# Four of twelve conditioning pieces scaled by ScalarE and summed by GpSimd in place of multiplied by TensorE

## The chip, the cores and the metric

The kernel runs on one core of a Trainium2 chip, in one launch. The metric is the device time of that launch in microseconds. Five engines work side by side and meet through semaphores: TensorE (matrix multiplication), VectorE, ScalarE, GpSimd, and SyncE (SP), which here only issues transfers. Each takes its own instructions in order.

## What is computed

A decoder layer over 512 tokens of width 1024, batch 1, all in float32:

```python
cond = silu(c)                                   # (1, 1024)
ada = cond @ w_ada + b_ada                       # (1, 6144)
sh1, sc1, g1, sh2, sc2, g2 = split(ada, 6)
h = rms_norm(x, norm1_g) * (1 + sc1) + sh1
q, ckv, qi, ki, wi, a_pool, gate_a, gate_b = split(h @ w_in)
o_a = sparse_attention(q, ckv, qi, ki, wi)       # top 128 keys of each query
o_b = multiscale_pool(a_pool, w_pool)
merged = sigmoid(gate_a) * (o_a @ w_a_up) + sigmoid(gate_b) * (o_b @ w_b_up)
x = x + g1 * (merged @ w_out)
h2 = rms_norm(x, norm2_g) * (1 + sc2) + sh2
x = x + g2 * moe(h2)                             # 4 of 32 experts
out = rms_norm(x, final_g)
```

The line that the change touches is `ada = cond @ w_ada`: one row times a 1024 x 6144 matrix. It is cut into twelve pieces of 512 columns, a0 to a11. Pieces 0 to 3 (shift and scale of the first norm) are needed at once; 4 to 11 make g1, sh2, sc2 and g2, which are used only after the attention stage. Pieces 8 to 11 are those changed.

## The kernel before

The work of every engine is written out by hand, in one list for each. TensorE's results go through the eight banks of PSUM: a list JOBS gives each result its number n and its bank n mod 8, and a job may start when the eighth job before it has been emptied (function start). An entry says who empties it, "A" ScalarE or "D" VectorE.

Weights of the first half come in pieces of 2 MB through four ring buffers in the order of PIECES, issued by SP. A piece is issued when the one before it in the same buffer has been used (function used). For a conditioning piece that is when its job is done. Because SP issues in order, a piece that waits holds all behind it. Around the change the order is a8, a9, gb1, a10, a11, wb (w_b_up), ga0, ga1, wa; a9, a10, a11 and ga0 share one buffer, and gb1 follows a8 in another.

The attention stage is a loop over eight groups g, two for each chunk of 128 queries (four heads each). In group g TensorE does, in this order: turned probabilities PT (L1617, four jobs), scores L of group g+1 (L1603), O(g) (probabilities times the latent, in L1480), the matmuls of gate part gb(g+1) (24 of them, in L1480), in group 0 the pooling product z (L1631), in odd groups V (L1480), in group 1 the row sums of pieces 4 to 7 (L1593), and in groups 0 to 3 a conditioning piece, ada_part(8 + g) at L1511. ScalarE copies the turned probabilities (L895) and O (L906), takes exponentials of group g+1 (L880), the tanh of the gate (L884), rounds the gate weights after the next into a high part (L821), and then copies z (L913), V (L916) and the conditioning result (L806). GpSimd makes the low part of those gate weights (L619); VectorE does the maxima (L1159), the top-k search, and scales the probabilities (L1193).

ada_part multiplies a piece with the conditioning vector in 8 matmuls, 32 columns wide, and leaves partial sums in 128 rows; a later sum over the rows with a matrix of ones (ada_sum) makes the row of 512 values, and ada_rows adds the bias. After the stage come the B branch, gate a with the A branch, the output projection, and the experts.

Of the kernel before, what the change touches and what calls it, by code (L numbers as in the profile page):

```python
# [24 lines left out]
ACT = mybir.ActivationFunctionType  # L25
# [5 lines left out]
KD = D // P  # L31
# [34 lines left out]
def trunk(nc, x, c, norm1_g, norm2_g, w_ada, b_ada, w_in, kv_norm_g, w_uk, w_uv, w_pool, pool_scale,  # L66
# [3 lines left out]
    with ctx:  # L70
# [3 lines left out]
        def sem(name):  # L74
            return ctx.enter_context(nc.semaphore(name))
# [12 lines left out]
        T3 = sb("T3", [P, 3, T])  # L88
# [16 lines left out]
        cnd = sb("cnd", [P, 3, KD])  # L105
# [159 lines left out]
        NGR = 2 * C  # L265
        JOBS += [("L", i, "D") for i in range(4)] + [("gb", 0, "A")]
        for g in range(NGR):
            JOBS += [("PT", 4 * g + i, "A") for i in range(4)]
            if g < NGR - 1:
                JOBS += [("L", 4 * g + 4 + i, "D") for i in range(4)]  # L270
            JOBS += [("O", g, "A")]
            if g < NGR - 1:
                JOBS += [("gb", g + 1, "A")]
            if g == 0:
                JOBS += [("z", i, "A") for i in range(PG)]
            if g % 2:
                JOBS += [("V", g // 2, "A")]
            if g == 1:
                JOBS += [("row", j, "D") for j in range(4, 8)]
            if g < 4:  # L280
                JOBS += [("ada", 8 + g, "A")]
        JOBS += [("B", m, "D") for m in range(KD)]
        JOBS += [("row", j, "D") for j in range(8, 12)]
        JOBS += [("ga", 0, "A")]
# [26 lines left out]
        zo_hi_ok, zo_lo_ok = sem("zo_hi_ok"), sem("zo_lo_ok")  # L311
        b_hi_ok, b_lo_ok = sem("b_hi_ok"), sem("b_lo_ok")
        c_ok = sem("c_ok")
        job_done = sem("job_done")
        by_act, by_vec = sem("by_act"), sem("by_vec")
        c_in, x_in, sv_in, kvg_in = sem("c_in"), sem("x_in"), sem("sv_in"), sem("kvg_in")
# [81 lines left out]
        def front_came(eng, kind, i=0):  # L398

            n = place[kind, i]  # L400
            eng.wait_ge(piece_in[slot_of[n]], 16 * (slot_of[:n + 1].count(slot_of[n])))
# [22 lines left out]
        def buffer_free(eng, kb):  # L424

            if turn_no[kb] >= 2:
# [3 lines left out]
                else:  # L430
                    eng.wait_ge(job_done, number[kind, m] + 1)

        def up_w_block(kind, m):
            return piece("wb" if kind == "B" else "wa")[:, :, m * P:(m + 1) * P]

# [14 lines left out]
        def _(sp):  # L450
# [6 lines left out]
            def used(n):  # L457

                kind, i, _ = PIECES[n]
                if kind == "a":  # L460
                    sp.wait_ge(job_done, number["ada", i] + 1)
                elif kind in ("wb", "wa"):
                    sp.wait_ge(u_lo_ok, KD if kind == "wb" else 2 * KD)
                elif kind in ("q", "pool", "gb", "ga"):
                    sp.wait_ge(b_lo_ok, block_no[LAST_JOB[kind, i]] + 1)
                else:
                    sp.wait_ge(job_done, number[LAST_JOB[kind, i]] + 1)
# [82 lines left out]
        def _(pool):  # L550
# [65 lines left out]
            def block_low(n):  # L616

                pool.wait_ge(b_hi_ok, n + 1)
                nc.gpsimd.tensor_tensor(wb_hl[:, buffer_of(BLOCKS[n]), 1, :, :], block_w(n),  # L619
                                        wb_hl[:, buffer_of(BLOCKS[n]), 0, :, :],  # L620
                                        ALU.subtract).then_inc(b_lo_ok, 1)
# [25 lines left out]
            for half in range(2):  # L647
                pool.dma_start(ada_half[half],
                               b_ada[0, 2 * D:6 * D].rearrange("(r a n) -> r a n", r=4, a=2)[:, half, :]
                               ).then_inc(brow_in, 16)  # L650
            for n in range(block_no["gb", 2], block_no["ga", 0]):
                block_low(n)
            pool.wait_ge(job_done, number["V", C - 1] + 1)

            for part in range(3):
# [117 lines left out]
        def _(act):  # L773
# [30 lines left out]
            def ada_copy(j):  # L804

                nc.scalar.activation(acc[j], job("ada", j), ACT.Copy).then_inc(by_act, 1)  # L806
# [65 lines left out]
            index_chunk(3)  # L872
            ada_copy(7)

            def exponentials(g):
                n = P * (g // 2 + 1)
                for i in range(4):
                    s = 4 * g + i
                    act.wait_ge(max_ok, s + 1)
                    nc.scalar.activation(Lt[:, i, 0:n], Lt[:, i, 0:n], ACT.Exp, scale=SCALE,  # L880
                                         bias=am[:, 1, s:s + 1], accum_out=am[:, 2, s:s + 1]).then_inc(exp_ok, 1)
# [8 lines left out]
            for g in range(NGR):  # L890
                ch, hh = g // 2, g % 2
                n = P * (ch + 1)
                for i in range(4):
                    src = job("PT", 4 * g + i)
                    nc.scalar.activation(pT[:, 0:ch + 1, i, :], src[:, 0:n].rearrange("p (s q) -> p s q", q=P),  # L895
                                         ACT.Copy).then_inc(by_act, 1)
                if g == NGR - 1:
                    act.wait_ge(job_done, number["L", 4 * NGR - 1] + 1)
                    for k in range(PG):
                        last = nc.scalar.activation(zo_hl[:, 0, k, :], zT[:, k, :], ACT.Copy)  # L900
                    last.then_inc(zo_hi_ok, 1)
                    up_high("B", 0)
                    up_high("B", 1)
                if g == 0:
                    act.wait_ge(d_ok, PG)
                nc.scalar.activation(o_latT[:, 4 * hh:4 * hh + 4, :].rearrange("p h q -> p (h q)"),  # L906
                                     job("O", g), ACT.Copy).then_inc(by_act, 1)
                if g < NGR - 1:
                    exponentials(g + 1)
                    gate_b(g + 1)  # L910
                if g == 0:
                    for i in range(PG):
                        nc.scalar.activation(zT[:, i, :], job("z", i), ACT.Copy,  # L913
                                             scale=svT[:, 24 + i:25 + i]).then_inc(by_act, 1)
                if hh:
                    nc.scalar.activation(oT[:, :, ch * P:(ch + 1) * P],  # L916
                                         job("V", ch).rearrange("p (a q) -> p a q", a=4),
                                         ACT.Copy).then_inc(by_act, 1)
                if g < 4:
                    ada_copy(8 + g)  # L920

            for m in range(2, KD):
                up_high("B", m)
# [122 lines left out]
        def _(dve):  # L1046
# [8 lines left out]
            def job(kind, i=0):  # L1055
                dve.wait_ge(job_done, number[kind, i] + 1)
                return bank(kind, i)

            v = nc.vector
# [81 lines left out]
            def ada_rows(j):  # L1141

                r, half = (j - 4) // 2, (j - 4) % 2
                row = small[32 * r:32 * r + 1, 1536 * half:1536 * half + CH]
                v.tensor_tensor(row, job("row", j)[32 * r:32 * r + 1, :], row, ALU.add).then_inc(by_vec, 1)

            last_scores = relu[:, 1, :]
# [309 lines left out]
        def _(pe):  # L1458
# [26 lines left out]
            def emptied_by(kind, i=0):  # L1485

                n = number[kind, i]
                pe.wait_ge(by_act if JOBS[n][2] == "A" else by_vec, emptied[n])
# [100 lines left out]
            def ada_sum(j):  # L1589

                b_ = start("row", j)
                emptied_by("ada", j)
                mm(b_, ones[:, :], acc[j], start=True, stop=True).then_inc(job_done, 1)  # L1593

# [15 lines left out]
            for g in range(NGR):  # L1611
                ch, hh = g // 2, g % 2
                for i in range(4):
                    b_ = start("PT", 4 * g + i)
                    pe.wait_ge(prob_ok, 4 * g + i + 1)
                    for s in range(ch + 1):
                        last = nc.tensor.transpose(b_[:, s * P:(s + 1) * P], Lt[:, i, s * P:(s + 1) * P], ident[:, :])  # L1617
                    last.then_inc(job_done, 1)
                if g < NGR - 1:
                    logits(g + 1)  # L1620
                b_ = start("O", g)
                emptied_by("PT", 4 * g + 3)
                chain(b_, [(ckv[:, s, :], pT[:, s, :, :].rearrange("p h q -> p (h q)")) for s in range(ch + 1)], job_done)
                if g < NGR - 1:
                    gate_b(g + 1)
                if g == 0:
                    pe.wait_ge(pool_in, 16)
                    for i in range(PG):
                        b_ = start("z", i)
                        pe.wait_ge(d_ok, i + 1)  # L1630
                        mm(b_, wpool[:, i, :], dT[:, i, :], start=True, stop=True).then_inc(job_done, 1)  # L1631
                if hh:
                    b_ = start("V", ch)
                    pe.wait_ge(uv_in, 16 * H)
                    emptied_by("O", g)
                    for a in range(4):
                        last = chain(b_[:, a * P:(a + 1) * P],
                                     [(uvp[:, 2 * a + q, :], o_latT[:, 2 * a + q, :]) for q in range(2)])
                    last.then_inc(job_done, 1)
                if g == 1:  # L1640
                    for j in range(4, 8):
                        ada_sum(j)
                if g < 4:
                    ada_part(8 + g)

            def branch(kind, m):

# [293 lines left out]
```

## Time and profile before

| | us |
|---|---|
| median of 3 runs | 997.53 (996.18 to 999.67) |
| the profiled execution, its own time | 998.4 |
| its span in the profile | 996.6 |
| TensorE busy | 956.7 (96%) |
| VectorE busy | 404.5 (41%) |
| ScalarE busy | 227.2 (23%) |
| GpSimd busy | 191.3 (19%) |

The span runs from the first to the last instruction of one execution; the 1.8 us around it are in the time but not in the span. Busy time of TensorE counts matmuls as they stream through and says little on how full they are. The attention stage lies between about 125 and 234 us of the span, the experts fill it from about 410 on.

### The profile page before, as it was taken

The page shows a single profiled execution, that of the slowest core. Times are in us where ns is not written, and L with a number is a line of the kernel's source. Part 1 is how long each engine was busy: PE and PEld are TensorE (multiplying, and loading weights), DVE is VectorE, ACT ScalarE, POOL GpSimd, SP SyncE. Part 2 cuts the span into 40 slices and gives each one's busy share as a digit, 9 for nine tenths or more (in the row PEclk, how much of TensorE's full clock was granted, in tenths as well). Part 3 has the DMA queues.
Part 4 walks back from the last instruction along what each step waited for, and adds up shares of the span by engine and source line. Part 5 has one row for each costly group of instructions (what it writes and reads, how often), then busy time and mean ns, then how long its engine had stood idle before and what let it go on. Part 6 is the DMA issues. An engine that isn't in the chain of part 4 may idle for free.

```text
span 996.6 us, 17022 instructions
## 1 busy us (share of the span) xinstructions
PE 956.7 (96%) x7199; PEld 517.7 (52%) x7199; DVE 404.5 (41%) x833; ACT 227.2 (23%) x488; POOL 191.3 (19%) x238
## 2 busy tenths in 40 slices
PE   3899989999999999899999999999999999999995
PEld 2676656767788746544444444443444444344442
DVE  0275967744533565323432323223232323223245
ACT  6334354443322323110010101011010101101012
POOL 2223941004200001212121111212111121211000
PEclk9999999999999999999999999999999999999998
DMA  9927623620422657989999999999999999999915
GB/s 338 341 86 253 229 84 122 242 85 16 170 85 96 242 231 262 349 301 375 377 348 372 390 387 385 389 386 397 372 397 385 388 389 379 386 370 393 381 37 182
DMA packets 71443, 283.96 MB, mean 285 GB/s; under 512 B 7488, under 2 KB 8796, under 8 KB 54984
## 3 DMA queue, kind: packets, MB, share of 16 engines
q1 hardware_dynamic: 61720, 257.93, 67.3%
q0 software_dynamic: 9648, 24.94, 9.5%
q8 instruction: 58, 0.95, 0.4%
q14 instruction: 17, 0.14, 0.0%
HBM read 272.62 MB, written 18.56 MB: 292 GB/s over the span
## 4 chain that ended last, share of the span: by engine, by line
PE 87%; DMA 5%; DVE 3%; issue 2%; ACT 1%; SPq 1%; POOL 0%; POOLq 0%; DVEq 0%; ACTq 0%
PE ps L1744 22%; PE ps L1480 20%; PE ps L1775 11%; PE ps L1755 11%; PE ps L1766 5%; PE ps L1692 2%; DMA ring<-in_w_ada_dram 2%; PE ps L1703 2%; PE ps L1731 2%; PE ps L1603 2%; PE ps L1532 2%; PE ps L1842 2%; PE ps L1511 1%; PE ps L1739 1%; DMA apad<-h_rows,iug 1%
## 5 line engine op out<-in xcount | busy, mean ns | idle before, releaser
L1317 DVE TENSOR_SCALAR mix<-ps 128x384 f32<-128x384 f32 x32 | 17.9, 558 | 288.3 <-ACT attn L980 288.3
L1480 PE MATMUL ps<-h_hi,wb_hl 128*128 128x512 f32 x384 | 126.0, 402 | 0.0
L700 POOL DMA_INDIRECT moe_rows<-mix,ius x31 | 47.8, 1543 | 249.4 <-DVE mix L1362 248.5
L1358 DVE SCALAR_TENSOR_TENSOR mix<-ps,WC,attn 64x512 f32<-64x512 f32 x64 | 47.9, 748 | 103.3 <-PE ps L1775 102.8
L980 ACT ACTIVATE attn<-ps 128x384 f32<-128x384 f32 x32 | 15.7, 491 | 309.1 <-PE ps L1755 309.1
L1480 PEld LDWEIGHTS ps<-h_hi,wb_hl 128*128 128x128 f32 x384 | 72.2, 188 | 19.7 <-issue 4.4
L1480 PE MATMUL ps<-h_lo,wb_hl 128*128 128x512 f32 x192 | 74.8, 389 | 0.0
L1362 DVE SCALAR_TENSOR_TENSOR mix<-ps,WC,attn 32x256 f32<-32x256 f32 x128 | 61.5, 481 | 1.9
L1744 PE MATMUL ps<-ring,mix 128*64 128x512 f32 x272 | 59.9, 592 | 0.0
L1744 PE MATMUL ps<-ring,uvp 128*64 128x512 f32 x256 | 59.0, 609 | 0.0
L619 POOL TENSOR_TENSOR wb_hl<-ring,wb_hl 128x1024 fp32r<-128x1024 f32 x16 | 38.5, 2415 | 85.1 <-ACT wb_hl L821 68.8
L1775 PE MATMUL ps<-ring,attn 128*64 128x512 f32 x240 | 54.8, 598 | 0.0
L992 ACT ACTIVATE attn<-ps 128x384 f32<-128x384 f32 x32 | 15.7, 491 | 168.2 <-PE ps L1842 168.2
L1480 PE MATMUL ps<-zo_hl,wb_hl 128*128 128x512 f32 x192 | 44.9, 389 | 0.0
L1480 PEld LDWEIGHTS ps<-h_lo,wb_hl 128*128 128x128 f32 x192 | 36.2, 189 | 9.1 <-issue 2.2
L1480 PEld LDWEIGHTS ps<-zo_hl,wb_hl 128*128 128x128 f32 x192 | 36.0, 188 | 7.4
L730 POOL COPY ius<-idx 128x1 uint32 (+1 forms) x31 | 7.8, 252 | 156.7 <-DMA moe_rows<-mix,ius 156.7
L1744 PEld LDWEIGHTS ps<-ring,mix 128*64 128x64 f32 x272 | 19.0, 137 | 35.3 <-issue 34.7
L694 POOL DMA_INDIRECT apad<-h_rows,iug x32 | 32.0, 999 | 25.2 <-POOL iug L721 24.4
L1744 PEld LDWEIGHTS ps<-ring,uvp 128*64 128x64 f32 x256 | 18.4, 141 | 34.7 <-issue 34.2
L821 ACT ACTIVATE wb_hl<-ring 128x1024 fp32r<-128x1024 f32 x24 | 25.2, 1052 | 38.5 <-PE ps L1480 32.6
L1775 PEld LDWEIGHTS ps<-ring,attn 128*64 128x64 f32 x240 | 15.9, 136 | 31.9 <-issue 31.9
(305 smaller groups left out, 1540.6 us busy)
## 6 DMA issues: line engine op xcount, KB each, us to landing
ring<-in_w_gu_dram SPq DMA_DIRECT2D x66, 1024.0 KB, 19.0
ring<-in_w_down_dram SPq DMA_DIRECT2D x30, 1024.0 KB, 13.5
ring<-in_w_ada_dram SPq DMA_DIRECT2D x12, 2048.0 KB, 11.9
area_b<-in_w_gu_dram SPq DMA_DIRECT2D x16, 1024.0 KB, 17.9
hT<-in_w_gu_dram SPq DMA_DIRECT2D x16, 1024.0 KB, 19.6
X<-in_w_gu_dram SPq DMA_DIRECT2D x16, 1024.0 KB, 18.9
area_a<-in_w_gu_dram SPq DMA_DIRECT2D x14, 1024.0 KB, 19.3
ring<-in_w_in_dram SPq DMA_DIRECT2D x6, 2048.0 KB, 7.9
```

The lines of the kernel that those rows point to most:

```text
L619: nc.gpsimd.tensor_tensor(wb_hl[:, buffer_of(BLOCKS[n]), 1, :, :], block_w(n), wb_hl[:, buffer_of(BLOCKS[n]), 0, :, :], ALU.subtract).then ...
L694: pool.indirect_dma_start(out=XG[0:slots, b, :], out_offset=None, in_=h2_dram, in_offset=bass.IndirectOffsetOnAxis(ap=iug[0:slots, b:b + 1 ...
L700: pool.indirect_dma_start(out=y_dram, in_=Y[0:slots, b, :], in_offset=None, out_offset=bass.IndirectOffsetOnAxis(ap=which, axis=0), bounds ...
L821: nc.scalar.activation(wb_hl[:, buffer_of(BLOCKS[n]), 0, :, :], block_w(n), ACT.Copy).then_inc(b_hi_ok, 1)
L1358: v.scalar_tensor_tensor(out=Y[0:SA, b, sl], in0=ps[SA * g:SA * (g + 1), 2, :], scalar=WC[0:SA, w:w + 1], in1=g2b[0:SA, sl], op0=ALU.mult, ...
L1362: last = v.scalar_tensor_tensor(out=Y[SA:slots, b, sl], in0=ps[SB * j:SB * (j + 1), 3, 0:2 * P], scalar=WC[SA:slots, w:w + 1], in1=g2b[SA: ...
L1480: last = mm(out_, a, b, start=(n == 0 and start_), stop=(n == len(pairs) - 1))
L1532: last = mm(b_[:, 0:TOKW], hT[:, k, ch * P:(ch + 1) * P], w[:, k, :], start=(k == 0), stop=(k == KD - 1))
L1744: mm(ps[SA * g:SA * (g + 1), 0, :], xgT[b][:, k, 0:SA], w[:, k % 2, g, :, :, :], start=False, stop=(k == KD - 1), tile_position=(0, SA * g))
L1755: last = mm(ps[SB * j:SB * (j + 1), 1, 0:2 * P], xgT[b][:, k, SA:slots], w[:, k % 2, j // 2, j % 2, :, :], start=False, stop=(k == KD - 1) ...
L1766: mm(ps[SB * j:SB * (j + 1), 3, 0:2 * P], actT[:, 2, SB * k:SB * (k + 1)], w[:, k % 2, 2 * P * j:2 * P * (j + 1)], start=(k == 0), stop=(k ...
L1775: last = mm(ps[SA * g:SA * (g + 1), 2, :], actT[:, k % 2, SA * (k // 2):SA * (k // 2) + SA], w[:, k % 2, g * CH:(g + 1) * CH], start=(k == ...
```

## The change

Pieces 8 to 11 are no longer multiplied by TensorE. Each consists of 8 parts of 128 x 512 (part k holds the rows of w_ada that partition p meets with value k of the conditioning vector). ScalarE multiplies a part by its column of the conditioning vector into one of two buffers in T3 (scale_parts), and GpSimd copies the first and adds the others into acc (add_parts). Scaling n waits until part n-2 has been added. In group 0 all eight parts of a8 are done, in each of groups 1 to 6 four parts. The sum over rows stays on TensorE, now waiting for GpSimd. The vector holds 1/32 of the values, so the row is multiplied by 32 in ada_rows.

```diff
-            if g < 4:
-                JOBS += [("ada", 8 + g, "A")]
...
+        SCALED = [[(8, k) for k in range(KD)]] + [[(9 + g // 2, 4 * (g % 2) + i) for i in range(4)] for g in range(6)]
+        scaled = [T3[:, 1 + i, :] for i in range(2)]
...
-                if kind == "a":
+                if kind == "a" and i >= 8:
+                    sp.wait_ge(scaled_ok, KD * (i - 7))
+                elif kind == "a":
                     sp.wait_ge(job_done, number["ada", i] + 1)
...
-            for n in range(block_no["gb", 2], block_no["ga", 0]):
-                block_low(n)
+            def add_parts(which):
+
+                for j, k in which:
+                    n = (j - 8) * KD + k
+                    pool.wait_ge(scaled_ok, n + 1)
+                    if k:
+                        pool.wait_ge(part_ok, n)
+                        last = nc.gpsimd.tensor_tensor(acc[j], scaled[k % 2], acc[j], ALU.add)
+                    else:
+                        last = nc.gpsimd.tensor_copy(acc[j], scaled[k % 2])
+                    last.then_inc(part_ok, 1)
+
+            block_low(block_no["gb", 2])
+            for g in range(NGR - 1):
+                if g + 3 < KD:
+                    block_low(block_no["gb", g + 3])
+                add_parts(SCALED[g])
...
+            def scale_parts(which):
+
+                for j, k in which:
+                    n = (j - 8) * KD + k
+                    front_came(act, "a", j)
+                    if n >= 2:
+                        act.wait_ge(part_ok, n - 1)
+                    nc.scalar.activation(scaled[k % 2], piece("a", j)[:, k, :], ACT.Copy,
+                                         scale=cnd[:, 2, k:k + 1]).then_inc(scaled_ok, 1)
...
+                if g < NGR - 1:
+                    scale_parts(SCALED[g])
                 if hh:
                     nc.scalar.activation(oT[:, :, ch * P:(ch + 1) * P],
                                          job("V", ch).rearrange("p (a q) -> p a q", a=4),
                                          ACT.Copy).then_inc(by_act, 1)
-                if g < 4:
-                    ada_copy(8 + g)
...
-                emptied_by("ada", j)
+                if j < 8:
+                    emptied_by("ada", j)
+                else:
+                    pe.wait_ge(part_ok, KD * (j - 7))
                 mm(b_, ones[:, :], acc[j], start=True, stop=True).then_inc(job_done, 1)
...
-                if g < 4:
-                    ada_part(8 + g)
```

ScalarE in the order of its list, before, from the gate of group 0 to the probability copies of group 2 (attn<-ps with 128x128 or 128x2x128 is L895; mix is the gate, wb_hl the high part, apad the V copy, area_b the z and conditioning copies):

```order
L884 ACTIVATE mix<-ps 128x512 [waits job_done]
L821 ACTIVATE wb_hl<-ring 128x1024 [waits job_done,piece_in0]
L913 ACTIVATE area_b<-ps,svT 128x512 [waits job_done] x4
L806 ACTIVATE area_b<-ps 128x512 [waits job_done]
L895 ACTIVATE attn<-ps 128x128 [waits job_done] x4
L906 ACTIVATE attn<-ps 128x512 [waits job_done]
L880 ACTIVATE attn,am<-attn,am 128x256 [waits max_ok] x4
L884 ACTIVATE mix<-ps 128x512 [waits job_done]
L821 ACTIVATE wb_hl<-ring 128x1024 [waits job_done,piece_in1]
L916 ACTIVATE apad<-ps 128x4x128 [waits job_done]
L806 ACTIVATE area_b<-ps 128x512 [waits job_done]
L895 ACTIVATE attn<-ps 128x2x128 [waits job_done] x4
```

The same place of ScalarE's list after the change (T<-ring,cnd is a scaling; line numbers have moved, L913 is the old L884, L924 the old L895):

```order
L913 ACTIVATE mix<-ps 128x512 [waits job_done]
L840 ACTIVATE wb_hl<-ring 128x1024 [waits job_done,piece_in0]
L942 ACTIVATE area_b<-ps,svT 128x512 [waits job_done] x4
L901 ACTIVATE T<-ring,cnd 128x512 [waits piece_in1] x2
L901 ACTIVATE T<-ring,cnd 128x512 [waits part_ok,piece_in1] x6
L924 ACTIVATE attn<-ps 128x128 [waits job_done] x4
L935 ACTIVATE attn<-ps 128x512 [waits job_done]
L909 ACTIVATE attn,am<-attn,am 128x256 [waits max_ok] x4
L913 ACTIVATE mix<-ps 128x512 [waits job_done]
L840 ACTIVATE wb_hl<-ring 128x1024 [waits job_done,piece_in1]
L901 ACTIVATE T<-ring,cnd 128x512 [waits part_ok,piece_in2] x4
L947 ACTIVATE apad<-ps 128x4x128 [waits job_done]
```

Eight scalings, and in later groups four, now stand ahead of the V copy and the probability copies; all but the first two wait for GpSimd (part_ok).

GpSimd before, from the end of pooling to the expert biases (wb_hl is the low part of the gate weights):

```order
L641 TENSOR_TENSOR area_b<-area_b,apad 128x512 [waits pool_chain]
L648 DMA small<-in_b_ada_dram 4x512 [waits job_done,select_ok]
L648 DMA small<-in_b_ada_dram 4x512
L619 TENSOR_TENSOR wb_hl<-ring,wb_hl 128x1024 [waits b_hi_ok] x6
L656 DMA T<-in_b_gu_dram 32x1024 [waits job_done]
```

GpSimd after, the same place (area_b<-T is the copy, area_b<-T,area_b the additions):

```order
L652 DMA small<-in_b_ada_dram 4x512
L623 TENSOR_TENSOR wb_hl<-ring,wb_hl 128x1024 [waits b_hi_ok] x2
L664 COPY area_b<-T 128x512 [waits scaled_ok]
L662 TENSOR_TENSOR area_b<-T,area_b 128x512 [waits part_ok,scaled_ok] x7
L623 TENSOR_TENSOR wb_hl<-ring,wb_hl 128x1024 [waits b_hi_ok]
L664 COPY area_b<-T 128x512 [waits scaled_ok]
L662 TENSOR_TENSOR area_b<-T,area_b 128x512 [waits part_ok,scaled_ok] x3
L623 TENSOR_TENSOR wb_hl<-ring,wb_hl 128x1024 [waits b_hi_ok]
L662 TENSOR_TENSOR area_b<-T,area_b 128x512 [waits part_ok,scaled_ok] x4
```

The six low parts stood alone in the list; now additions stand between them, and a group's low part comes ahead of its additions.

## Rows read from the trace of the kernel before

**Rows 1.** The page's first part: busy us, share of the span, instructions.
```profile
PE 956.7 (96%) x7199; PEld 517.7 (52%) x7199; DVE 404.5 (41%) x833; ACT 227.2 (23%) x488; POOL 191.3 (19%) x238
```
**Rows 2.** Busy us by stretch of the span, attention stage; then PEclk, DMA share, GB/s.
```profile
core 0: us, PE busy (x) PEld busy (x) DVE busy (x) ACT busy (x) POOL busy (x), PEclk, DMA share, GB/s
140.00:230.00 90.00, 89.01 (x425) 59.34 (x424) 52.83 (x164) 42.78 (x106) 15.46 (x8) 1.00 0.40 141
```
**Rows 3.** The chain that ended last, attention stage: start us, us, what.
```profile
142.22 1.85 PE ps L1511 x16
...
144.66 1.73 PE ps L1603 x8
146.39 8.13 PE ps L1480 x42
...
162.56 7.18 PE ps L1480 x28
169.74 1.85 PE ps L1511 x16
...
175.20 8.96 PE ps L1480 x44
...
190.06 8.05 PE ps L1480 x30
198.11 1.31 PE ps L1617 x12
...
202.85 9.81 PE ps L1480 x46
...
217.85 8.93 PE ps L1480 x32
226.80 0.60 ACT mix L884
...
229.50 3.69 PE ps L1480 x8
```
**Rows 4.** ScalarE in order of time: start us, us, engine, line, what [idle before].
```profile
140.26 1.84 ACT L913 ACTIVATE area_b<-ps,svT 128x512 f32<-128x512 f32 x3
...
144.63 0.78 ACT L895 ACTIVATE attn<-ps 128x128 f32<-128x128 f32 x4
...
169.78 0.60 ACT L884 ACTIVATE mix<-ps 128x512 f32<-128x512 f32 x1 [2.90 <-PE ps L1480]
170.27 1.05 ACT L821 ACTIVATE wb_hl<-ring 128x1024 fp32r<-128x1024 f32 x1
...
172.15 1.21 ACT L895 ACTIVATE attn<-ps 128x256 f32<-128x256 f32 x4
...
227.30 2.06 ACT L895 ACTIVATE attn<-ps 128x512 f32<-128x512 f32 x4
```
**Rows 5.** GpSimd in order of time, group 0.
```profile
144.02 4.72 POOL L619 TENSOR_TENSOR wb_hl<-ring,wb_hl 128x1024 fp32r<-128x1024 f32 x2
```
**Rows 6.** Three lines of GpSimd: duration ns min/median/max, first and last start, forms.
```profile
L641 POOL TENSOR_TENSOR area_b<-area_b,apad x4: 1272/1297/1600, 103.4 to 129.4; 128x512 f32<-128x512 f32 x4
L635 POOL TENSOR_TENSOR attn<-attn x6: 1039/1041/1264, 108.2 to 127.1; 128x512 f32<-128x512 f32 x6
L639 POOL TENSOR_SCALAR area_b<-attn x4: 607/607/872, 102.7 to 128.7; 128x496 f32<-128x496 f32 x4
```
**Rows 7.** Transfers issued from 138 to 230: KB each, median us to landing.
```profile
ring<-in_w_in_dram SPq DMA_DIRECT2D x3, 2048.0 KB, 7.8
```
**Rows 8.** TensorE in order of time ahead of group 0.
```profile
127.30 0.30 PE L1617 MATMUL ps<-ident,attn 128*128 128x128 f32 x1 [2.11 <-DVE attn L1193]
128.56 0.70 PE L1617 MATMUL ps<-ident,attn 128*128 128x128 f32 x2 [0.96 <-DVE attn L1193]
```
**Rows 9.** TensorE by stretch: us, busy, granted clock, DMA share, GB/s.
```profile
130.00:140.00 10.00, 10.00 (x38) 0.83 0.01 2
420.00:430.00 10.00, 9.32 (x36) 0.66 1.01 381
```
**Rows 10.** VectorE in order of time, group 1.
```profile
154.72 2.25 DVE L1193 TENSOR_SCALAR attn<-attn,am 128x256 f32<-128x256 f32 x1
```

More of the change, by code:

```diff
@@ L313, in trunk @@
         c_ok = sem("c_ok")
+        part_ok, scaled_ok = sem("part_ok"), sem("scaled_ok")
         job_done = sem("job_done")
@@ L1144, in ada_rows @@
                 row = small[32 * r:32 * r + 1, 1536 * half:1536 * half + CH]
-                v.tensor_tensor(row, job("row", j)[32 * r:32 * r + 1, :], row, ALU.add).then_inc(by_vec, 1)
+                v.scalar_tensor_tensor(out=row, in0=job("row", j)[32 * r:32 * r + 1, :], scalar=(32.0 if j >= 8 else 1.0),
+                                       in1=row, op0=ALU.mult, op1=ALU.add).then_inc(by_vec, 1)
             last_scores = relu[:, 1, :]
```

## Prediction

> **What bounds the kernel now.** I read the busy shares first: TensorE is busy 956.7 of 996.6 us [rows 1], and 89.01 of the 90 us between 140 and 230, where the attention stage lies [rows 2]. A busy share alone does not say that TensorE sets the end, so I read the chain that ended last through this stage [rows 3]: from 142 on its pieces are TensorE work, and only at 226.80 does ScalarE come into it. So TensorE time taken out here comes off the end, and a wait goes onto it. After the stage the order of work is fixed and its weight loads are released by the same jobs, so I take a shift of the stage as a shift of the end, one for one.
>
> Then the two engines that get the work. ScalarE is busy 42.78 of those 90 us and GpSimd 15.46 [rows 2]: by totals there is room. What counts is where in a group the work stands, since both take their instructions in order. In group g, ScalarE finishes the gate of group g+1 (L884, then the high part L821) and then copies the turned probabilities (L895), and TensorE cannot start O without these copies. The time from the end of the gate matmuls to O is where the change will be felt; I call it the turnaround. For O(3) it is 169.74 to 175.20, 5.46 us: 1.85 for a conditioning piece, 3.6 for transposes and scores [rows 3].
>
> **What is removed.** Four multiplications of a conditioning piece, 1.85 us each on the chain [rows 3]: 7.4 us. Four copies of their results on ScalarE go too; ScalarE was waiting for TensorE there, so I count nothing.
>
> **What is added, and its prices.** 32 scalings on ScalarE of 128x512 with a scale per partition. The nearest row is L913 (from PSUM, same shape, same kind of scale), three in 1.84 us, each overlapping the next [rows 4]; I take 0.55. On GpSimd 28 additions of 128x512 and 4 copies. The addition reads two different tiles and writes one of them, as L641 does (median 1.297); L635 reads one tile twice and takes 1.041 [rows 6]. I take 1.29 plus 0.08 between dependent instructions, 1.37, and 1.13 as the low end. The f32 copy is not in the trace: L639, a one-input form of 496 elements, takes 0.607 [rows 6]; I take 0.75 with its gap.
>
> The Trainium skill, GPSIMD Engine Reference, sections 3.1 and 4.1, speaks against this move: it sends two-input elementwise work to VectorE because GpSimd pays about 2.6 cycles an element. An estimate from that page, 512 elements at 1.2 GHz, is 1.11 us, between the two rows; with it (and the same gap) the sum below would be 2.3 us smaller.
>
> **The hold.** There are two scaling buffers, so the third scaling of a group waits for the first addition, the fourth for the second. GpSimd begins each group up to 4 with its own low part L619, 2.4 us [rows 5], which waits for the same high part. And the scalings stand ahead of the next probability copies on ScalarE. So behind the waiting scaling are queued the V copy and the four L895 copies, hence O, hence the next gate on TensorE. On SP the gb1 piece, and all behind it, now waits for the eighth scaling.
>
> Group 0 has eight parts. GpSimd does two low parts from 144.02 to 148.74 [rows 5], the copy to 149.5, then an addition every 1.37: the sixth part ends at 156.35. The eighth scaling waits for it and ends at 157.05; four copies (0.78 [rows 4]) end at 157.8, and O(1) starts at 157.95. It was 146.39 [rows 3]: **+11.6**, the removed multiplication of this group already in it.
>
> For the others I set the new turnaround against the old. Group 2 to O(3): from the gate's end 0.12 to ScalarE, gate copy 0.5, high part 0.95 (from the starts and durations at 169.78 and 170.27 [rows 4]), low part 0.1 + 2.4, two additions 2.74, 0.1 + 0.55 for the last scaling, copies 4 x 0.30, 0.15 to TensorE: 8.8. Old 5.46: **+3.35**. Group 4 to O(5): the copies are 4 x 0.41 (between 0.30 at width 256 and 0.515 at 512 [rows 4]), so 9.25; old 202.85 - 198.11 = 4.74 [rows 3]: **+4.5**. Group 6 to O(7): no low part, no scores. 0.12 + 0.5, scalings with their waits 0.55 + 0.1 + 2.74 + 0.1 + 0.55 = 4.04, copies 2.06, 0.15: 6.9. The old gate ended about 226.7 and O began at 229.50, 2.8: **+4.1**.
>
> Odd groups have the V turn, about 1.85, which covers part. O plus gate took 7.18 from O(2) and 8.05 from O(4) [rows 3], which gives the ends of the odd gates: 152.7, 182.4, 210.9. Group 3 to O(4): here the first part is the shorter copy, so the last scaling ends 6.85 after the gate; V copy 0.5, copies 1.64, 0.15: 9.15. Old 190.06 - 182.4 = 7.7: **+1.5**. Group 1 to O(2): again 6.85 and V copy 0.5; then one transpose that needs the bank of V (with the ada jobs gone, the eighth job before it is V), 0.33, and scores 1.73 [rows 3]: 9.4. The gb1 piece, released at 157.1 and not at 144.07, lands 8 to 8.5 later (7.8 in the trace [rows 7]) and holds the high part 0.7 more: 10.1. Old 162.56 - 152.7 = 9.9: **+0.25**. Group 5 to O(6): no low part, copies ready after 6.75; TensorE itself took 217.85 - 210.9 = 6.95: **0**.
>
> Sum: 11.6 + 0.25 + 3.35 + 1.5 + 4.5 + 0 + 4.1 = **+25.3**, the saved 7.4 included. On this path lie 13 additions (5, 1, 2, 1, 2, 0, 2), so 0.1 us on one moves the end 1.3.
>
> **The clock.** TensorE waited 2.11 and 0.96 us around 127 to 129 [rows 8], and the granted clock then averaged 0.83 from 130 to 140: 3.4 us at the lower level (1.2 GHz), a loss of 1.7. Around 420 the mean was 0.66 over ten, 6.8 us at that level, a loss of 3.4 [rows 9]. After the change TensorE waits 13.4 us before O(1) (scores done at 144.5), and 5.2, 4.5 and 5.1 before O(3), O(5) and O(7). I take the smaller loss four times, 6.8, since it lies in this stage, less the 0.7 of the gb1 piece, which the slower matmuls hide: **+6.1**. The ends of this term are 0 and 13.
>
> 25.3 + 6.1 = +31.4. On the profiled execution's 998.4 us that is 1029.8; the median of the three runs is 997.53, 0.9 lower, so I forecast **1029 us**.
>
> **Costed at nothing.** The row sum at L1145 gets another form of the same size, off the chain. The a10, a11 and ga0 loads are each released one or more groups later, but each has 13 us or more until its use; a load over that would add its excess once. w_b_up is issued behind a11 and has about 25 us.
>
> **Rivals.**
> *It fits by totals.* 32 scalings are 17.6 us against 47 idle on ScalarE, the additions 41 against 74 idle on GpSimd [rows 2]; TensorE stays the bound and gains 7.4: 990.1. Group 2 decides: TensorE needs 3.6 for transposes and scores, ScalarE 2.9 without a hold, so a hold under 0.7 costs nothing and one over 2.5 eats the saving. I count 5.9. Even free additions would leave group 0 with six scalings behind the low parts: O(1) at 153.1, +6.7. Chance 0.02; no change 0.01.
> *The hold without the clock.* The waits stand, but the clock drops once or not at all: 1019.5 (25.3 less 3.1 for quick additions) to 1025. Only two drops stand in the trace, so that each wait brings one is not shown. Chance 0.22.
> *Contention.* One probability scaling on VectorE took 2.25 us, its neighbours about 0.35, while a GpSimd subtraction ran [rows 10]. Meeting GpSimd's additions could do this in each group, or stretch the additions: at 1.6 each the sum is 13 x 0.23 = 3 more, 1032. Against it: GpSimd adds right behind the gate, when VectorE is past these scalings. With four clock losses of 3.4 it is 1036. Chance 0.2 for both.
> *The likeliest*, four waits with four short drops, 1025 to 1033: 0.55.
>
> The Trainium skill, Advanced Engine Details and Errata, VectorE Performance Modes, Mode Summary, notes that VectorE's second port is shared with GpSimd and that two-port forms and GpSimd block each other. The 2.25 us row agrees.
>
> The range 1018 to 1038 takes in quick additions without a clock loss and the long clock losses. A difference under 0.3% could not be told from none here: slower 0.97, same 0.01, faster 0.02.
>
> **What would show it.** Right: TensorE waits for the probability copies about 13 us before O(1) and 4 to 6 before O(3), O(5), O(7), about none before O(6); ScalarE waits for GpSimd's additions; additions of about 1.3; clock at the lower level for some us after these waits. Wrong: additions far from 1.3, no wait before O(5) and O(7), a wait over 2 us on a late piece, or later stages that take part of the shift back.

## The result and the profile after

| | median us | lowest to highest | ratio to before, 95% interval |
|---|---|---|---|
| before, same chip | 997.6 | 996.2 to 999.7 | |
| after | 1041.0 | 1039.2 to 1044.4 | 1.0435 [1.0409, 1.0462] |

The change costs 43.4 us. I had forecast 1029, with 1038 as the upper end: the sign was right, and 12 us were missing. The profiled execution took 1044.43 us, 46 more than the one of before, so I look for some 46 us in the trace.

First the page's busy shares of after, as in [rows 1]: busy us, share of the span, instructions.
```profile
PE 966.9 (93%) x7135; PEld 523.4 (50%) x7135; DVE 403.9 (39%) x833; ACT 245.7 (24%) x516; POOL 227.2 (22%) x270
```
TensorE has 64 matmuls fewer and is still busy 10 us longer; the lower granted clock shown below accounts for it. The other 36 us of the span are waits and stops. No engine got full: ScalarE gained 18.5 us and GpSimd 35.9, and both are still mostly idle.

The waits of TensorE in the attention stage of after: who waited for whom, us in total, times, longest.
```profile
PE ps L1510 <- ACT attn L924: 28.9, 5, 13.5
PE ps L1636 <- ACT apad L947: 2.3, 1, 2.3
PE ps L1650 <- ACT apad L947: 1.5, 1, 1.5
PE ps L1510 <- ACT attn L935: 0.8, 1, 0.8
```
L924 is the probability copy (L895 of before), L947 the V copy, L1510 the products of O, L1636 the scores and L1650 the transposes; the last row, V(3) behind the copy of O(7), is 0.8 in the kernel before too. Where the waits stand shows in TensorE's own order of time (after; start us, us, what, in brackets the idle time ahead and its releaser). These are the starts of O(1), O(3), the late scores of group 3, and O(4) to O(7):
```profile
159.01 2.05 PE L1510 MATMUL ps<-attn,ckv 128*128 128x512 f32 x2 [13.52 <-ACT attn L924]
192.57 3.75 PE L1510 MATMUL ps<-attn,ckv 128*128 128x512 f32 x4 [5.14 <-ACT attn L924]
209.23 0.91 PE L1636 MATMUL ps<-T,hT 128*128 128x384 f32 x2 [2.31 <-ACT apad L947]
210.84 5.46 PE L1510 MATMUL ps<-attn,ckv 128*128 128x512 f32 x6 [0.70 <-ACT attn L924]
231.22 5.46 PE L1510 MATMUL ps<-attn,ckv 128*128 128x512 f32 x6 [4.39 <-ACT attn L924]
249.29 3.60 PE L1510 MATMUL ps<-attn,ckv 128*128 128x512 f32 x8
265.27 6.75 PE L1510 MATMUL ps<-attn,ckv 128*128 128x512 f32 x8 [5.15 <-ACT attn L924]
```
O(1), O(3), O(5) and O(7) wait for the copies, O(6) doesn't. Eight products of O take 3.60 us at O(6) and 6.75 at O(7): same work, at half the clock (the granted clock from 265 to 272 is 0.54).

The chain that ended last says what the copies were late for. Group 0 of after:
```profile
147.48 2.30 POOL wb_hl L623
149.78 0.56 POOL area_b L664
...
150.47 1.28 POOL area_b L662
...
151.89 1.28 POOL area_b L662
...
156.12 1.27 POOL area_b L662
...
157.48 0.72 ACT T L901
158.20 0.68 ACT attn L924 x4
...
159.01 8.16 PE ps L1510 x26
```
Where [rows 3] had TensorE alone, there now stand GpSimd's low part (L623), its copy (L664), five additions (L662), ScalarE's eighth scaling (L901) and its four copies. The additions start 1.41 us apart, 1.27 of it busy.

The clock behind three of the waits, by stretch (after; us, TensorE busy, granted clock as a share of 2.4 GHz, DMA share, GB/s):
```profile
190.00:195.00 5.00, 2.43 (x3) 0.50 0.43 131
195.00:200.00 5.00, 5.00 (x19) 0.86 0.79 288
210.00:215.00 5.00, 4.30 (x6) 0.50 0.01 3
215.00:220.00 5.00, 5.00 (x18) 0.81 0.00 0
230.00:235.00 5.00, 3.79 (x5) 0.55 0.78 253
235.00:240.00 5.00, 5.00 (x16) 0.77 1.01 369
```
From each start of O until its matmuls quicken, TensorE runs at 1.2 GHz: 3.2 us at O(1), 3.8 at O(3), 6.8 from the late scores of group 3 on, 6.1 at O(5), 6.2 at O(7). Half of each is lost: 1.6, 1.9, 3.4, 3.0 and 3.1, together 13.0 us.

The last piece lies nowhere near the change. TensorE ahead of its last 16 matmuls (the last expert's combine), before:
```profile
979.95 7.11 PE L1914 MATMUL ps<-mix,small 128*128 128x512 f32 x16 [0.52 <-DVE mix L1362]
```
and after:
```profile
1023.77 9.81 PE L1945 MATMUL ps<-mix,small 128*128 128x512 f32 x16 [4.59 <-issue]
```
A stop of 4.6 us, where it was 0.5, that no semaphore explains ("issue"), then 2.7 us more for the same matmuls: 6.8 us in all.

**The balance.** From the start of z to group 7's V products the stage took 95.3 us before and 133.1 after, +37.7; it began 1.1 later in this execution. Up to the reading of the last rows (977.54, now 1017.01) the shift is 39.5, up to the first output write (986.82, now 1032.89) 46.1. So the long expert stage gives nothing back, and the tail adds 6.6. In the stage TensorE's waits add up to 32.7 (the rows above and the 1.5 at L1650), where before had one of 1.0 ahead of O(7); less that and the 7.4 of the removed multiplications it is 24.3. Of the 37.7 then 13.4 are left for the clock; the stretches gave 13.0.

### The profile page after: what moved, and what is told of

Read it like the earlier page. It is cut to its first block, busy times and chain, and to the rows that moved or that the text cites. A ratio compares the mean times of both kernels' runs of the same rounds, so it can differ in the third digit from the quotient of the medians.

```text
span 1042.7 us, 17008 instructions
## 1 busy us (share of the span) xinstructions
PE 966.9 (93%) x7135; PEld 523.4 (50%) x7135; DVE 403.9 (39%) x833; ACT 245.7 (24%) x516; POOL 227.2 (22%) x270
## 4 chain that ended last, share of the span: by engine, by line
PE 81%; issue 5%; POOL 4%; DMA 4%; DVE 3%; ACT 2%; SPq 1%; DVEq 0%; POOLq 0%; ACTq 0%
PE ps L1775 21%; PE ps L1510 18%; PE ps L1806 11%; PE ps L1786 10%; PE ps L1797 5%; PE ps L1723 2%; POOL area_b L662 2%; PE ps L1762 2%; DMA ring<-in_w_ada_dram 2%; PE ps L1734 2%; PE ps L1562 2%; PE ps L1873 1%; POOL wb_hl L623 1%; DMA apad<-h_rows,iug 1%; PE ps L1770 1%
## 5 line engine op out<-in xcount | busy, mean ns | idle before, releaser
L1510 PE MATMUL ps<-h_hi,wb_hl 128*128 128x512 f32 x384 | 129.0, 410 | 0.0
L1510 PEld LDWEIGHTS ps<-h_hi,wb_hl 128*128 128x128 f32 x384 | 73.7, 192 | 21.2 <-issue 5.5
L1510 PE MATMUL ps<-h_lo,wb_hl 128*128 128x512 f32 x192 | 75.6, 394 | 0.0
L1510 PE MATMUL ps<-attn,ckv 128*128 128x512 f32 x40 | 30.9, 926 | 28.9 <-ACT attn L924 28.9
L623 POOL TENSOR_TENSOR wb_hl<-ring,wb_hl 128x1024 fp32r<-128x1024 f32 x16 | 38.4, 2407 | 83.3 <-ACT wb_hl L840 66.3
L1510 PE MATMUL ps<-zo_hl,wb_hl 128*128 128x512 f32 x192 | 44.9, 389 | 0.0
L1510 PEld LDWEIGHTS ps<-h_lo,wb_hl 128*128 128x128 f32 x192 | 36.9, 192 | 10.4 <-issue 3.3
L1510 PEld LDWEIGHTS ps<-zo_hl,wb_hl 128*128 128x128 f32 x192 | 35.9, 188 | 7.4
L662 POOL TENSOR_TENSOR area_b<-T,area_b 128x512 f32<-128x512 f32 x28 | 35.5, 1267 | 14.6 <-ACT T L901 11.0
## 6 DMA issues: line engine op xcount, KB each, us to landing
ring<-in_w_gu_dram SPq DMA_DIRECT2D x66, 1024.0 KB, 18.5
```

Of the source, the lines that this page charges most:

```text
L662: last = nc.gpsimd.tensor_tensor(acc[j], scaled[k % 2], acc[j], ALU.add)
L1510: last = mm(out_, a, b, start=(n == 0 and start_), stop=(n == len(pairs) - 1))
```

## The experiments

T in the expectations is the theory that GpSimd's additions hold ScalarE and so O, and that the clock behind the waits costs the rest. Medians are compared with runs of the kernel before on the same chip; "stage" is the stretch from the start of z to group 7's V products, 95.3 us before. hum issues short bf16 matmuls whose results nobody reads, 0.12 to 0.13 us each. In the last four expectations T is another theory, which each of them states.

**Again.** The changed kernel, unaltered.

> The changed kernel once more, for its profile. Theory T (the hold: probability copies queued behind scalings that wait for GpSimd, plus clock losses of 13 us, plus a tail of up to 6 us): the waits before O(1), O(3), O(5), O(7) are again 13.5, 5.1, 4.4 and 5.1 us within 0.3, since they follow from fixed durations; the stretches at the lower clock differ by some us in place and length; the wait of 4.6 us of TensorE before the last 16 matmuls either stands again (then it belongs to the program) or is near 0.5 (then it varies by execution). Time 1037 to 1045. Rival (the waits themselves vary, for instance through transfers): one of the four waits differs by more than 1 us.

Measured: 1040.3, ratio 1.0416 [1.0377, 1.0455]; the waits before O are 13.51, 5.12, 4.39 and 5.15, the stage takes 133.0, the stop ahead of the combine 4.8, and the matmuls behind it 8.58 where they had taken 9.81. Waits, drops and the stop belong to the program, not to one execution; the clock behind the stop varies.

**Short matmuls in the waits.** If the clock falls because TensorE idles, work without a use should keep it up.
```diff
+                hum(b_, {1: 100, 3: 36, 5: 30, 7: 36}.get(g, 0))
```
This stands directly ahead of O(g), in O's own bank.

> The changed kernel with short matmuls without use in TensorE's waits before O(1), O(3), O(5), O(7) (100, 36, 30, 36 of about 0.12 us). The waits stay as long as they are, so only the clock changes. Theory T (the lower clock behind the waits costs 13 us, 3.4 of it behind the wait at O(4), which is not filled): 9 to 10 us less, 1031, and a granted clock near 1.00 from 159 to 200. Rival (the clock term is what I predicted, 6 us, and the remainder is something else): 4 to 5 us less, 1036.

Measured: 1044.6, ratio 1.0454 [1.0412, 1.0496]; no gain, where I had expected 1031. The trace says why (TensorE, in order of time):
```profile
158.13 12.95 PE L1506 MATMUL ps<-ones,onesb 128*128 128x256 bf16 x100 [12.93 <-ACT attn L924]
...
278.54 3.70 PE L1510 MATMUL ps<-attn,ckv 128*128 128x512 f32 x8 [1.14 <-ACT attn L924]
```
O's bank is the one that the probability copy empties, so the short matmuls waited for the same copy and then came on top: 12.95, 5.77 and 6.25 us in groups 1, 3 and 5. Only those of group 7, whose bank was free, lay in the wait, and there the eight products of O took 3.70 instead of 6.75. The stage is 143.6 us, 10.6 longer than in the repeat; the time doesn't show it because the stop ahead of the combine is 0.5 us in this kernel. So I put the others into a bank that VectorE had long emptied:
```diff
+                    if g == 5 and i == 3:
+                        pe.wait_ge(by_vec, emptied[number["L", 4 * g]])
+                        hum(bank("L", 4 * g), 12)
...
+                if g in (1, 3, 5):
+                    pe.wait_ge(by_vec, emptied[number["L", 4 * g + 4]])
+                    hum(bank("L", 4 * g + 4), {1: 100, 3: 30, 5: 24}[g])
...
+                if g == 7:
+                    hum(b_, 38)
```

> The changed kernel with matmuls without use in all five waits of TensorE (before O(1) 100, O(3) 30, the last score ahead of O(4) 12, O(5) 24, O(7) 38, 0.12 us each), now in a bank that VectorE has just emptied, so that they stand inside the waits. In the run before, three of the four groups of them had waited for the probability copies themselves, and only those before O(7) filled a wait: there the clock stayed at 1.00 and O(7) to V took 4.5 us, not 7.5. Theory T (13.0 us are lost to the lower clock in the stage: 1.6, 1.9, 3.4, 3.0, 3.1): the V of group 7 starts 11 to 13 us earlier, at 260 to 262 and not 272.8, clock near 1.00 from 160 on; the time 1026 to 1031, by the wait near the end. Rival (the clock follows its own course, whatever TensorE does in the waits): V at 268 or later.

Measured: 1023.3, ratio 1.0248 [1.0224, 1.0272], less than the 1026 to 1031 expected. The clock by stretch, in this kernel:
```profile
150.00:160.00 10.00, 7.36 (x67) 0.97 0.01 2
160.00:170.00 10.00, 10.00 (x44) 0.86 0.60 210
170.00:180.00 10.00, 8.54 (x33) 1.00 0.01 2
...
200.00:210.00 10.00, 8.30 (x53) 1.00 0.01 4
...
220.00:230.00 10.00, 8.22 (x39) 1.00 0.31 98
```
All drops but the first are gone, and the stage is 122.4 us, 10.6 less than in the repeat, though the copies come no sooner (O(1) starts 19.3 us behind z in both). The rest of the gain of 17 us fits the tail: here the combine comes after 0.5 us. So the clock was worth about 11 us with one drop of 1.4 (10 us at 0.86) left: 12 in all.

**Additions ahead of the low part on GpSimd.**
```diff
+                add_parts(SCALED[g])
                 ...
-                add_parts(SCALED[g])
```
The first stands ahead of block_low, the second behind it.

> The changed kernel with GpSimd's additions of a group ahead of its low part (in group 0 one low part still comes first). Theory T (the hold holds the low part's 2.4 us): 2.4 less before O(1), 1.9 less before O(2) to O(5) each, about 9.6 in all, and up to 3 more where a shorter wait no longer lowers the clock: V of group 7 at 260 to 264, 1028 to 1033. Rival (the low part would run beside the first scalings anyway and adds nothing): less than 3 us.

Measured: 1023.1, ratio 1.0258 [1.0240, 1.0275], the stage 116.6; 5 us less than the low end of what I expected. The waits are 11.21, 3.46, 0.59 with 0.70, 2.69 and 5.15, and none is left before O(2): 8.9 us less. The gain in the stage is 16.5, since between 170 and 240 the clock never falls either, behind these shorter waits:
```profile
180.00:190.00 10.00, 6.54 (x26) 1.00 0.20 68
...
210.00:220.00 10.00, 7.31 (x28) 1.00 0.23 70
```
The hold is GpSimd's, and its low part was 9 us of it. The 7.6 us beyond that are what the shorter waits gave back of the clock, more than twice the 3 us that I had allowed for.

**No additions.** GpSimd only copies the last part; the other seven of each piece stay out of the sum, and ScalarE waits for nothing of GpSimd's but that one copy of a piece.
```diff
+                    if k < KD - 1:
+                        continue
+                    pool.wait_ge(scaled_ok, KD * (j - 7))
+                    nc.gpsimd.tensor_copy(acc[j], scaled[1]).then_inc(part_ok, 1)
...
-                        act.wait_ge(part_ok, n - 1)
+                        act.wait_ge(scaled_ok, n - 1)
```

> The changed kernel with the additions left out: GpSimd copies only the last scaled part of each piece, so the four rows are sums over one part in eight; the 32 scalings stay where they are and wait for none of GpSimd's work but one copy a piece. Theory T (the wait for the additions is the cost, the scalings' own time the rest): the holds shrink to 4 x 0.63 (8 x 0.63 in group 0): O(1) near 150.5 after scores at 145.3, O(3), O(5), O(7) with waits of 2 to 3, at most one or two clock drops: 1003 to 1009. Rival (scalings on ScalarE in themselves cost most): over 1020.

Measured: 1007.5, ratio 1.0109 [1.0076, 1.0142], the stage 102.5. What is left are the scalings themselves, which stand ahead of the probability copies on ScalarE: 4.25 us of wait before O(1), 1.71, 0.50, 0.94 and 3.42 before O(3), O(4), O(5) and O(7).
```profile
148.60 2.04 PE L1508 MATMUL ps<-attn,ckv 128*128 128x512 f32 x2 [4.25 <-ACT attn L922]
```
So ScalarE's waiting for GpSimd, for its low part as well as its additions and with the clock that this costs, is 30.6 of the stage's 37.7 us. The waits left are 10.8 us, 1.0 of them there before. That alone is 2.4 more than the 7.4 saved, and the remaining 4.8 of the 7.2 us by which this stage is still longer than before are left for the clock. A kernel with eight scaling buffers in place of two, which would have shown what the hold costs with all additions still made, has no room in SBUF beside the other tensors and was not measured.

**The four pieces left out.** The kernel before, without their multiplications and copies; the row sums then go over other data, and SP issues the load behind each of these pieces when it has landed and a gate part is done (not shown).
```diff
-            if g < 4:
-                JOBS += [("ada", 8 + g, "A")]
...
-                if g < 4:
-                    ada_copy(8 + g)
...
-                if g < 4:
-                    ada_part(8 + g)
```

> The kernel before with the multiplications of pieces 8 to 11 and their copies left out and nothing in their place; the pieces are still loaded, and the four rows are sums over other data. It prices what is taken from TensorE alone. Theory (TensorE is the bound in groups 0 to 3): 4 x 1.85 = 7.4 less, less 0.5 to 1 where the probabilities come late: 991 (990 to 993), if the end of the kernel is as before. Rival (VectorE's search is nearly the bound, so most of the saving turns into waits for probabilities): 994 to 996, with waits of TensorE for L1193 of 3 us or more.

Measured: 996.7, ratio 0.9987 [0.9968, 1.0006], where I had expected 991 with an unchanged end. The stage is 6.3 us shorter (7.4 saved, with a new wait of 1.3 for GpSimd's low part), but the end has changed:
```profile
974.74 9.83 PE L1912 MATMUL ps<-mix,small 128*128 128x512 f32 x16 [5.46 <-issue]
```
The stop at the tail has come with it, into a kernel that puts nothing of these pieces on ScalarE or GpSimd. So it is no matter of the scalings. All five kernels with the stop (after, its repeat, the additions first, no additions, the pieces left out; 4.2 to 5.5 us) have 64 matmuls and 64 weight loads fewer than before: everything behind stands 128 instructions earlier. The two with short matmuls in the waits, which have about 200 matmuls more, don't have it. The next three runs test that place in the program.

**64 short matmuls at the start.** One line at the program's start (they run from 2.0 to 11.1 us, while the first loads are under way) puts the 128 instructions back; applied to after, before, and the kernel without the pieces.
```diff
+            hum(bank("sv"), 64)
```

> The changed kernel with 64 short matmuls without use at the very start of TensorE's list, where TensorE waits for the first transfers, which costs nothing there; it moves all later instructions by 128 places. Theory T (part of the change's cost is where its instructions fall against the blocks in which they are loaded): the wait falls to 0.5, the matmuls behind it run at the upper clock, and the time falls by 4 to 7 us, to 1034 to 1037. Rival (the wait is a result of what the engines do at the end, or of the clock): the wait stays over 4 us and the time within 1 us.

> The kernel before with the same 64 short matmuls at the start. Removing pieces took 128 instructions from the list and brought the wait near the end; if blocks are 256 instructions long, adding 128 puts the end at the same place within a block. Theory T: the wait of 4 to 5.5 us appears in the unchanged kernel, 4 to 7 us slower, 1002 to 1005. Rival (the pads' position means nothing): no change, the wait at 0.5.

> The kernel with pieces 8 to 11 not multiplied (rows are sums over other data) and 64 short matmuls at the start. Its stage was already 6.4 us shorter, its time only 1.0 us less, with a wait of 5.5 near the end. Theory T: the wait falls to 0.5 and the time to 990 to 992, which shows the full price of the removed multiplications. Rival: stays at 995 to 997.

| | without, us (ratio to before) | with 64, us (ratio to before) | stop ahead of the combine, us |
|---|---|---|---|
| after | 1041.0 [1.0409, 1.0462] | 1034.5 [1.0342, 1.0394] | 4.6, then 0.5 |
| before | 997.3 | 1002.9 [1.0035, 1.0076] | 0.5, then 4.6 |
| without the pieces | 996.7 [0.9968, 1.0006] | 988.2 [0.9881, 0.9925] | 5.5, then 0.5 |

The first and third kernel were measured without the 64 at another time than with them, so compare the ratios, each to before on the same chip; the intervals don't touch. More work made two of the kernels 6 and 8 us faster, and the unchanged one 6 slower; the stages stayed at 133.1, 95.3 and 89.0. The first two times lie where I had expected them, the third 2 us below. Before with 64 more, the same row as above:
```profile
985.67 10.16 PE L1915 MATMUL ps<-mix,small 128*128 128x512 f32 x16 [4.61 <-issue]
```
The DMA queue that carries instructions shows what falls in that time. The row is that of after from 1021 to 1022, one packet of 0.02 MB, inside its stop (1019.2 to 1023.8):
```profile
q8 instruction: 1, 0.02, 6.0%
```
In before with 64 more it comes in 982 to 983, inside the stop too; in the plain kernel before in 971 to 972, while TensorE still had the last expert's matmuls to do, and there is no stop. The other traces agree: in all six kernels with the stop such a packet moves inside it, and in all six without it the packet comes 7 to 9 us ahead of the last matmuls. (The Trainium skill, Advanced Engine Details and Errata, ISA Cache, gives a cache line as 16 KB, 256 instructions, which fits packets of 0.02 MB.) That the place in the program switches the stop on and off is shown; that TensorE stands still for this packet is read from its time alone, and wasn't tested apart.

**Interleaved.** A version from all this: a8 stays on TensorE; of a9 to a11 two scalings stand behind the probability copies and two behind the copy of O in each of groups 1 to 6; additions ahead of the low part; 48 short matmuls at the start.
```diff
+            if g == 0:
+                JOBS += [("ada", 8, "A")]
...
+        SCALED = [[]] + [[(9 + g // 2, 4 * (g % 2) + i) for i in range(4)] for g in range(6)]
...
+                if g < NGR - 1:
+                    scale_parts(SCALED[g][0:2])
...
+                    scale_parts(SCALED[g][2:4])
...
+            hum(bank("sv"), 48)
```

> A version built on what the runs showed: a8 stays on TensorE; a9 to a11 are scaled by ScalarE and added by GpSimd in groups 1 to 6, four parts each, but two scalings stand between the probability copies and the copy of O and two behind that copy, where ScalarE waits anyway; GpSimd adds ahead of its low part; 48 short matmuls at the start keep the later instructions where they are in the kernel before. Theory T (the cost was the place, not the work): no wait of TensorE for probability copies over 0.5 us but the old one before O(7), 3 x 1.85 = 5.5 less, some 0.5 to 1 lost to probabilities that come late: 992 to 994. Rival (GpSimd's additions now meet VectorE's probability scalings and hold them, as the 2.25 us row): scalings over 1 us in several groups, 995 to 999.

Measured: 992.0 (990.8 to 993.3) beside 997.3, ratio 0.9941 [0.9921, 0.9961]: faster than both kernels, than the one before by only 0.6%, which is clear of the noise. As in the kernel before, the combine comes after 0.5 us. The stage takes 90.6, 4.7 less than before, for three multiplications of 1.85. TensorE's waits for ScalarE in the stage are two, both also there before:
```profile
PE ps L1515 <- ACT attn L926: 1.0, 1, 1.0
PE ps L1515 <- ACT attn L939: 0.8, 1, 0.8
```
24 scalings and 21 additions are still made. For these three pieces the place decides; the fourth, whose eight parts made the wait of 13.5 us, went back to TensorE. The order on GpSimd, changed here too, had alone left the stage at 116.6.

## Why the prediction was wrong

**What bounds the kernel; the hold.** Right, in place and size. Forecast waits of 13.4, 5.2, 4.5 and 5.1 before O(1), O(3), O(5) and O(7), and none before O(6); measured 13.52, 5.14, 4.39, 5.15 and none. O(1) was forecast at 157.95; it came at 159.01 in an execution whose stage began 1.1 later. Turnaround by turnaround, waits less work taken out, the forecast was 11.6, 0.25, 3.35, 1.5, 4.5, 0 and 4.1, and the chip gave 11.67, -0.39, 3.29, 1.16, 4.39, 0 and 4.16: 24.3 against 25.3. The prices: the f32 copy took 0.60, and 0.75 with its gap, as taken; the pitch of the additions was 1.41, not 1.37 (1.27 busy; the estimate of 1.11 from the Trainium skill, GPSIMD Engine Reference, section 3.1, was too low, like the 1.04 row of [rows 6]); the last scaling of a group 0.72, and 0.63 until the next copy starts, not 0.55. Two prices were a little too low and no turnaround but O(2)'s is off by more than 0.35, so small errors must offset each other in the sums; that part of the agreement is luck.

**The gb1 piece.** It was issued at 158.22 instead of 144.13, as forecast, but ScalarE didn't wait for it. O(2)'s delay came from the V copy alone (1.46 us before its transposes), and of the seven turnarounds this one erred most, by 0.6.

**The clock: the failed term.** I took "the smaller loss four times", +6.1 with the 0.7 off, and the chip showed 13.0, the other end of the term. Two things were wrong in it. The single loss of 1.7 came from [rows 9], where TensorE had waited 2.11 and 0.96; four of the five drops here lost 1.9 to 3.4. And I counted drops by waits for the copies over 4 us: in group 3 the two waits of 2.31 and 0.70 brought a fifth, the costliest, of 3.4. My own [rows 8] should have told me so: 2.11 and 0.96 had done it there. The 0.7 taken off had nothing to stand on either, since the gb1 piece held nothing.

**The shift of the end: the second failure.** "I take a shift of the stage as a shift of the end, one for one" left out the last 25 us; a term that I had put at nothing was 6.5 us. The removed matmuls move every later instruction of TensorE, and in this kernel that costs a stop of 4.6 us (0.5 before) ahead of the last 16 matmuls and 2.7 us of clock in them. Without it (after with 64 short matmuls) the time is 1034.5, 1.5 above the likeliest case of 1025 to 1033 and inside the range up to 1038. Neither failure alone would have left the range (1029 and 7 more for the clock, or 6.5 more for the tail, is 1036); together they did.

**Rivals.** "It fits by totals" fell at O(1), where the first wait stands. "The hold without the clock" fell with the five drops. Of "contention", additions weren't slowed (1.27 of the 1.29 assumed), and no probability scaling on VectorE took over 0.49; its other half, long clock losses, was the true one, but at 1036 it lacked the tail. Three terms now make up the 43.4 us: 24.3 for waits less work saved, 13 for the clock, and 6.5 for the tail by the pair of runs with and without the 64 (together 43.8).

## What to carry over

Idle time on an engine is worth nothing to a stage if the work lands ahead of something that the bound engine waits for: put the same work behind it, one or two parts at a time, and it may become a gain (992 here, against 997 before and 1041 after the change). Price each new wait of TensorE twice: as a wait, and as a loss of clock behind it. That loss was 1.6 to 3.4 us here, also for waits of 3 us in all, and nothing behind the waits of 2.7 and 3.5 us in the run with the additions first, so it is a range and not a price. And when instructions are added or taken out, look at the program's end for a stop without a releaser before explaining a few us by the edit: some short matmuls at a harmless place tell the two apart.

## What the runs showed of the hardware

- **A stop that the place in the program switches.** The stop ahead of the combine takes 4.2 to 5.5 us with "issue" as its releaser, and the next 16 matmuls take 8.6 to 10.2 us instead of 7.1; 128 instructions far ahead switch it: 997.3 to 1002.9, 1041.0 to 1034.5, 996.7 to 988.2. A late block of instructions is the likely cause, not a shown one.
- **No sharp price of a wait.** Waits of 2.69 and 3.46 us left the clock at 2.4 GHz (additions ahead of the low part), waits of 3.42 and 4.25 (no additions) and of 2.31 with 0.70 (after) brought 1.2 GHz. What TensorE did between the waits differed; I can't say which of it decides.
- **VectorE beside GpSimd.** In the interleaved kernel one probability scaling took as long as that of [rows 10], and three others took about three times their usual time. VectorE in order of time, group 1, and GpSimd's low part beside it:
```profile
156.87 0.35 DVE L1228 TENSOR_SCALAR attn<-attn,am 128x256 f32<-128x256 f32 x1
157.33 2.33 DVE L1228 TENSOR_SCALAR attn<-attn,am 128x256 f32<-128x256 f32 x1
157.17 2.35 POOL L625 TENSOR_TENSOR wb_hl<-ring,wb_hl 128x1024 fp32r<-128x1024 f32 x1 [1.43 <-ACT wb_hl L842]
```
  The slow scaling ends at 159.66, 0.14 us behind the low part. In groups 3, 5 and 6 one took 1.23, 1.40 and 1.55 where its neighbours took 0.42 to 0.49; these began while GpSimd added and ended 0.2 to 0.3 us behind the additions. So such a meeting costs VectorE what is left of GpSimd's instruction, up to 2.0 us here; TensorE didn't wait for it. This agrees with the Trainium skill (Advanced Engine Details and Errata, VectorE Performance Modes), by which the second port of VectorE is shared and the two engines block each other.
